# Two contraction steps in a row per token tile in the second feed-forward product of an encoder layer

## The reference

```
u = rmsnorm(h, norm_g[l, 2])
f = jnp.square(jax.nn.relu(u @ w_ff1[l])) @ w_ff2[l]
h = h + rmsnorm(f, norm_g[l, 3])
```

## Time and profile before

| what | value |
|---|---|
| median of 3 runs | 1398.29 us (1398.01 to 1399.68) |
| the profiled execution | 1399.42 us |
| its span, first to last instruction | 1397.7 us |
| PE busy | 1370.8 us (98%) |
| DVE busy | 989.5 us (71%) |
| ACT busy | 600.6 us (43%) |
| matmuls of line 1136 | 1344, first start at 1084.1, last at 1391.4 us |
| granted TensorE clock, mean | 0.997 of full speed |

### The profile page before, as it was taken

The page is one execution under the profiler, slowest core; times in us unless marked ns, Lnnn a source line. Parts: engine busy times, 40 slices in busy tenths (PEclk is TensorE's granted clock), DMA queues, the critical chain, the costliest instruction groups (busy, mean ns, idle before and its releaser), DMA issues.

```text
span 1397.7 us, 17147 instructions
## 1 busy us (share of the span) xinstructions
PE 1370.8 (98%) x6209; PEld 1116.8 (80%) x6209; DVE 989.5 (71%) x1425; ACT 600.6 (43%) x929; POOL 112.5 (8%) x73
## 2 busy tenths in 40 slices
PE   7999999999999999899999999999999999999998
PEld 6778777777778788688888888888888778888886
DVE  7787796886989754466566787676665597765676
ACT  6544544544544444501243453333332354444454
POOL 0000000000000000000000323333323100000000
PEclk9999999999999999999999999999999999999999
DMA  5111111101111332354732155444445964336343
GB/s 185 46 31 31 30 31 30 45 15 38 37 30 54 109 117 90 110 157 150 253 105 75 53 179 189 137 155 155 144 158 188 382 215 148 98 108 209 106 129 112
DMA packets 141613, 162.02 MB, mean 116 GB/s; under 512 B 6829, under 2 KB 88938, under 8 KB 141418
## 3 DMA queue, kind: packets, MB, share of 16 engines
q1 hardware_dynamic: 135392, 148.14, 33.2%
q10 hardware_dynamic: 6154, 13.01, 2.4%
HBM read 114.98 MB, written 46.14 MB: 115 GB/s over the span
## 4 chain that ended last, share of the span: by engine, by line
PE 85%; DVE 6%; DMA 4%; ACT 2%; issue 2%; ACTq 0%; SPq 0%; DVEq 0%
PE psum L866 34%; PE psum L983 23%; PE psum L1136 19%; PE psum L904 2%; PE psum L1113 2%; PE psum L949 2%; DMA f_raw<-f_scratch 2%; PE psum L953 1%; DVE g_sum L1862 1%; DMA gates_scratch<-staging 1%; DMA w_raw<-in_w_in 1%; ACT staging L1291 1%; PE psum L1085 1%; DVE w_lo L1686 0%; DVE dev L1828 0%
## 5 line engine op out<-in xcount | busy, mean ns | idle before, releaser
L1136 PE MATMUL psum<-op 128*128 128x512 f32 x1344 | 305.6, 389 | 2.1 <-DVE op L2170 2.0
L1136 PEld LDWEIGHTS psum<-op 128*128 128x128 f32 x1344 | 252.1, 188 | 55.5 <-issue 3.3
L866 PE MATMUL psum<-act_hi,w_hi 128*128 128x512 f32 x448 | 182.0, 406 | 1.1 <-DVE act_lo L1680 1.1
L866 PE MATMUL psum<-act_hi,w_lo 128*128 128x512 f32 x448 | 175.2, 391 | 0.0
L866 PE MATMUL psum<-act_lo,w_hi 128*128 128x512 f32 x448 | 174.6, 390 | 0.0
L2167 DVE TENSOR_TENSOR op<-v,op 128x512 fp32r<-128x512 f32 x112 | 78.5, 700 | 85.0 <-ACT op L1541 84.8
L1541 ACT ACTIVATE op<-v 128x512 fp32r<-128x512 f32 x112 | 70.6, 631 | 139.1 <-PE psum L1136 125.1
L866 PEld LDWEIGHTS psum<-act_hi,w_hi 128*128 128x128 f32 x448 | 84.2, 188 | 21.3 <-issue 3.4
L866 PEld LDWEIGHTS psum<-act_lo,w_hi 128*128 128x128 f32 x448 | 84.3, 188 | 18.0 <-issue 1.9
L866 PEld LDWEIGHTS psum<-act_hi,w_lo 128*128 128x128 f32 x448 | 84.1, 188 | 18.2
L2170 DVE TENSOR_TENSOR op<-f_raw,op 128x512 fp32r<-128x512 f32 x112 | 77.8, 695 | 17.4 <-ACT op L1543 17.4
(11 more groups left out here) (265 smaller groups left out, 2802.6 us busy)
## 6 DMA issues: line engine op xcount, KB each, us to landing
f_raw<-f_scratch SPq DMA_DIRECT2D x112, 256.0 KB, 2.7
w_raw<-in_w_in SPq DMA_DIRECT2D x34, 512.0 KB, 4.7
w_raw<-in_w_ff SPq DMA_DIRECT2D x32, 512.0 KB, 5.0
f_scratch<-f_out SPq DMA_DIRECT2D x56, 256.0 KB, 2.4
gates_scratch<-staging ACTq DMA_DIRECT2D x32, 256.0 KB, 2.0
gate_in<-gates_scratch SPq DMA_DIRECT2D x16, 512.0 KB, 4.3
v<-in_w_ff SPq DMA_DIRECT2D x8, 1024.0 KB, 8.5
v<-in_w_ff SPq DMA_DIRECT2D x4, 2048.0 KB, 12.1
```

The costliest lines, as they stand in the source:

```text
L866: mm = nc.tensor.matmul(bank, stat(a, kt), moving(b, kt), start=(n == 0), stop=(n == len(terms) - 1))
L1136: mm = nc.tensor.matmul(psum[:, (X_BANK, Z_BANK)[m % 2][t]], op[n % SLOTS][:, 2 + a, token_cols(t)], op[n % SLOTS][:, b], start=(m in (0, ...
```

## The change

The loop over contraction steps now goes by pairs. A token tile takes both steps of a pair (six matmuls into its bank) before the next tile follows. The waits for the operands of both steps stand ahead of the pair. `step_done` still rises once per step, with the step's last matmul on the last tile. The last product has 13 steps ahead of its tail, so its last group is a single step.

```
             for m in range(len(KEPT)):
                 last = m == len(KEPT) - 1
-                for kt in range(STEPS - TAIL if last else STEPS):
-                    operands(m * STEPS + kt)
+
+                count = STEPS - TAIL if last else STEPS
+                for first in range(0, count, 2):
+                    pair = range(first, min(first + 2, count))
+                    for kt in pair:
+                        operands(m * STEPS + kt)
                     for t in range(HT):
-                        if kt == 0:
+                        if first == 0:
                             y_bank(m, t)
-                        mm = y_step(m, kt, t)
-                    mm.then_inc(step_done, 1)
+                        for kt in pair:
+                            mm = y_step(m, kt, t)
+                            if t == HT - 1:
+                                mm.then_inc(step_done, 1)
```

## The result

The changed kernel takes 1403.44 us, median of 7 runs (1402.34 to 1405.63), against 1398.29 us (1398.01 to 1399.68, 7 runs) before. The ratio is 1.0034 with a 95% interval of 1.0023 to 1.0045: 5.1 us slower, clear of noise. A second comparison of the same two kernels gave 1.0044 (1.0030 to 1.0057).

The account below looks back on a forecast made before the run. PE, busy 98% of the span, was taken as the bound, with DMA deciding until step 14. Terms 2.72 + 2.2 + 0.2 = 5.1 us on the median 1398.29 gave 1403.4 us, range 1400.6 to 1405.6.

Parts of the forecast that it names:

- Steps 10 to 13: Start of the changed loop: step 10 waits for step 11's late f block; PE 2.72 us behind in total.
- (12, 13): a gap of 1.2 us as before: Pair after (10, 11): PE waits 1.2 us as before, ready at 1122.27 us; not a second loss.
- Part 2: Steps 10 and 11: 2.72 us lost; SP's loads about 3.1 us later, hidden by more than 6 us of queued work.
- Steps 68 and 69: h loads delayed 2.04 us beside the general 2.72; new wait of 2.1 us plus 0.1 restart, 2.2 us taken.
- the lower bound's reason: Step 69's wait: DMA engines, at share 0.87, may catch up so the landing doesn't follow the 2.04 us; 0.1 us remains.
- Steps 88 and 98: `finish_rows` between even and odd step: twice 0.03 us and a 0.1 us restart each, 0.2 us, between 0 and 0.6.
- Steps 14 to 63: PE leads and four slots suffice: no cost, 1.4 us left at two sums of v behind each step.
- Fewer bank changes: Matmul stream: 216 of 436 bank changes removed, at most 1.0 us gained; nothing booked.
- only the first wait costs: Rival: step 69's f block comes in time; 1401.1 us, chance 0.12.
- nothing shows: Rival: blocks of 11 and 13 less late in most executions, 69 in time; 1398.3 to 1399.5 us, chance 0.06.
- faster: Rival: matmul stream quicker with fewer bank changes, each worth 36 ns or more; under 1395.5 us, chance 0.04.
- More waits: Rival: DVE's chain longer than reckoned, or DMA queue runs dry, 11 and 13 later; 1404.6 to 1408 us, chance 0.12.

Follow-up runs that it names:

- e2: Changed kernel with the fifth block product (steps 64 to 79) step by step again, the others in pairs; 1.0030 against the kernel before.
- e3: Changed kernel with the first and fifth block products step by step again, the other five in pairs; 1.0009 against the kernel before.
- e7: Changed kernel with the eight h loads behind the f block of step 69 rather than 68; 1.0024 against the kernel before.
- e8: Changed kernel with the two 2 MB v loads behind the f blocks of steps 11 and 13; 1.0023 against the kernel before.
- e1: Changed kernel with the first block product (steps 0 to 15) step by step again, the others in pairs; 1.0025 against the kernel before.
- e6: Kernel before with the two 2 MB v loads behind the f blocks of steps 11 and 13, not 10 and 12; 0.9986 against the kernel before.
- e9: Kernel before with the two 2 MB v loads behind the f blocks of steps 11 and 14; 0.9983 against the kernel before.
- e5: Changed kernel with pairs beginning at odd steps, (1, 2) to (13, 14), 0 and 15 alone; 1.0022 against the kernel before.
- e4: Changed kernel with the odd step's wait moved behind the even step's first three matmuls on tile 0; 1.0025 against the kernel before.

## Why the prediction was right

It gave 1403.4 us and the measured median is 1403.44. So close a hit is partly luck: the interval of the ratio is 3 us wide, and terms that were off cancelled (2.7, 2.2 and 0.2 us in the sum; 3.0, 1.7 and 0.3 in the first profile, 2.9, 2.2 and 0.3 in the third). But the two places that it named carry the loss, and e2, e3, e7 and e8 each removed what they were meant to remove.

**Steps 10 to 13** (2.72 us): the even step does stand behind its neighbour's late block, and the loss becomes final at step 14, as worked out. What "(12, 13): a gap of 1.2 us as before" missed is that this gap wasn't there in any of the three profiles of the changed kernel. PE ran slowly behind the first gap, and that filled the second and 0.3 to 0.4 us more in the first profile: its operands were ready at 1122.63 + 0.69 + 0.15 = 1123.47, but ACT's start on step 14 at 1123.34 puts the end of step 10 at 1123.14, and the pair's end three matmuls later, at 1123.8. Step 14 starts at 1129.26 against 1125.09 before; less the 1.20 by which the blocks landed later, the term is 2.97. At full clock it is the 2.72 of the sum: e2, whose clock stayed up, shows 2.7 and both gaps, the one ahead of (12, 13) at the forecast 1.2 us (1.07 on PE's record). So the slow matmuls cost only about 0.25 us net. The gap ahead of (10, 11), forecast at 2.7 us, was 2.2 to 2.4 from start to start less a matmul; its size depends on how early PE arrives, and nothing in the sum hangs on it. The cover held that Part 2 relied on: SP issued step 10's block at 1099.50 us against 1095.68 before, and step 11's block landed no later, counted from the loop's start (28.9 us against 29.9). (By Part 2's own terms the load moves by 1.2 + 2.04 = 3.2 us, not 3.1; nothing rests on it.) The wait ahead of (2, 3), put at 1.2 us, was 0.49 to 1.32 us on PE's record and hidden in every profile, as forecast.

**Steps 68 and 69** (2.2 us): the h loads moved by 6.21 us. Of these, 1.20 are the chance shift of this execution's DMA stretch and 0.25 the slow matmuls, which leaves 4.76, the 2.72 + 2.04 reckoned. The third profile of the changed kernel shows the wait at its largest:

```profile
1114.10 159.54 PE L1136 MATMUL psum<-op 128*128 128x512 f32 x696 [2.15 <-DVE op L2176]
1275.62 113.67 PE L1136 MATMUL psum<-op 128*128 128x512 f32 x499 [1.98 <-DVE op L2176]
```

The last matmul of the first piece starts at 1114.10 + 159.54 - 0.39 = 1273.25, the next 2.37 us later, where 0.23 is normal: 2.1 us lost, and 0.1 for the restart, the 2.2 of the sum. The same difference was 1.6 us in the first profile and 1.7 in the second, with the restart 1.7 and 1.8. In the first profile the block landed about half a microsecond less late than if it had followed fully. Whether the DMA engines caught up in part, the lower bound's reason, isn't shown: this landing wanders by itself. In the second profile of the kernel before it came at 1269.42 against 1270.54, while step 11's block came only 0.4 us earlier.

**Steps 88 and 98** (0.2): from step 70 to the last matmul the changed kernel takes 0.3 us more than the one before, about 0.15 at each of the two waits. **Steps 14 to 63** (nothing): right for the changed kernel, but my reason was too good. I had put 1.4 us to spare at two sums per step for any pair; e3 and e1 show that at (16, 17) the room came from the time that PE had already lost. **Fewer bank changes** (nothing): steps 14 to 59 have 184 changes of bank in the kernel before and 92 in the changed one, and take 125.12 us in both, 0.2267 a matmul. So fewer changes gain nothing. The rule of the Trainium skill ("TensorE: Matmul & The Clock Gate", "HAM oscillation — how this bites in real kernels"), that all contraction steps of a tile ahead of a wait for data keep the clock up, turned out the other way here: the grouping made the wait longer, and of the four profiles with the former order (before twice, e6, e9) none has a stretch at a lowered clock in this loop. The prediction's sentence that no run shows a lowered clock overlooked the trace of before ahead of this loop, where the granted clock is 0.64 from 590 to 595 us; that stretch is no part of the change.

The rivals: "only the first wait costs" is refuted by the gap at 68, "nothing shows" and "faster" by the ratio. "More waits" (DVE or a dry queue) was wrong for the changed kernel, though its mechanism, DVE at two sums per step, is real in e3.

## What to carry to other kernels

Grouping steps replaces several waits by one for the latest operand and holds the earlier slot longer. So look first for the steps whose operands arrive with little or nothing to spare, and ask which of them would become the second of a group. With a ring of four slots, pairs leave half the lead. Where a large load stands ahead of a small, urgent one in the same queue, try exchanging the two: in the former kernel that gave 2.0 to 2.4 us and left no gap (e9). In the changed one it moved part of the loss to the next pair (e8).

## What the runs showed of the hardware that was not expected

**Slow matmuls behind a gap of over 2 us.** In the changed kernel's three profiles, and in e7, the stretch behind the gap ahead of (10, 11) has a lowered granted clock: 0.62 in 1117 to 1121 us of the first, where PE was busy throughout with 12 matmuls in 4 us, 0.67 and 0.70 in 1112 to 1117 us of the second and third, 0.76 in 1117 to 1121 us of e7. The two levels are 1.2 and 2.4 GHz; 0.62 over the window is a part of it at the low one: seven matmuls start 0.43 us apart there rather than 0.227. Ahead of it PE had worked at full clock since the last gap and then stood still for 2.6 us on the weight loads' record. e2 had the same gap at the same place (2.25 us on PE's record), and its clock stayed up, 20 matmuls in the same 4 us:

```profile
1117.00:1121.00 4.00, 4.00 (x20) 3.29 (x19) 1.99 (x4) 0.00 (x0) 0.00 (x0) 1.00 1.05 386
```

In e5 a gap of 2.80 us at 1089.77 left it at 1.00 as well, and so did gaps of 1.94 (e4, ahead of step 11), 1.98 and 2.03 us (third profile and e1, ahead of step 68). The four with slow matmuls behind them were 2.05 to 2.22 us on the same record. So the length of the gap alone doesn't decide, and what does is not settled here. The slow matmuls of the first profile take about 1.6 us longer, and since they ran into the wait ahead of (12, 13) that would have come anyway, only about 0.25 us of it was lost.

**A start that wanders.** The changed loop begins at 1082.7 to 1086.3 us over 14 profiles, without regard to the edit. This is as large as most effects measured here, so a single profiled execution can't rank such edits by its span. The length of the loop can't quite either: it wanders by 1 us and more with the landing of step 11's block. Counted from that landing, the kernel before gives 277.4 us twice and the changed one 282.5, 282.5 and 282.9.
